# A tenth 2 MB home for the expert weights in a hybrid attention/RWKV/MoE step, with the residual reloaded elsewhere

## The reference, cut to what matters

```python
x = x + mixed @ w_out                                  # residual 1, after attention + RWKV-7 branches
h = rmsnorm(x, ln2)
logits = h @ w_router + b_router ; top 4 of 32 experts, softmax over the 4
for each expert e:
    gu = h_e @ w_gate_up[e] + b_gate_up[e]             # 1024 x 2048 weights, 8 MB
    act = (clip(up) + 1) * (min(gate, 7) * sigmoid(1.702 * min(gate, 7)))
    y_e = act @ w_down[e] + b_down[e]                  # 1024 x 1024 weights, 4 MB
x = x + sum of gate_e * y_e
y = rmsnorm(x, ln_f)
```

## Time and profile before

| what | value |
|---|---|
| runs | 1280.0, 1279.75, 1284.23 us |
| the profiled execution's own time | 1278.74 us |
| its span in the profile | 1276.9 us |
| granted TensorE clock, mean | 0.998 of full speed |
| PE busy | 1204.8 us (94%) |
| bytes moved | 458.76 MB |

### The profile page before, as it was taken

One profiled execution on the slowest core, in us unless ns is written; L12 is line 12 of the kernel. 1 busy time (PEld: TensorE's weight loads), 2 busy tenths in 40 slices (PEclk: granted clock), 3 DMA queues, 4 the chain that ended last, 5 costly groups with the idle time before them and its releaser, 6 DMA issues.

```text
span 1276.9 us, 18583 instructions
## 1 busy us (share of the span) xinstructions
PE 1204.8 (94%) x7592; PEld 590.1 (46%) x7592; DVE 339.3 (27%) x655; ACT 208.3 (16%) x421; POOL 87.0 (7%) x64
## 2 busy tenths in 40 slices
PE   6999999999999999999998989999898989898997
PEld 5877789875543433434333333324242433333332
DVE  1068497566411111111111111011111111111102
ACT  3133253320310110111011001000110101010002
POOL 0161003711000000000000000000000000000001
PEclk9999999999999999999999999999999999999999
DMA  9879450158699999999999999999999999999994
GB/s 318 196 249 300 141 210 12 37 191 339 272 379 428 428 427 429 428 426 428 428 429 425 429 428 427 427 428 429 427 428 428 428 428 428 427 428 427 428 427 185
DMA packets 52656, 458.76 MB, mean 359 GB/s; under 512 B 7092, under 2 KB 10844, under 8 KB 28004
## 3 DMA queue, kind: packets, MB, share of 16 engines
q1 hardware_dynamic: 49972, 452.22, 86.2%
q0 software_dynamic: 1824, 5.12, 1.7%
q10 hardware_dynamic: 784, 0.28, 0.1%
HBM read 453.74 MB, written 3.82 MB: 358 GB/s over the span
## 4 chain that ended last, share of the span: by engine, by line
PE 60%; DMA 29%; DVE 6%; ACT 2%; POOL 1%; issue 1%; SPq 0%; DVEq 0%; ACTq 0%; POOLq 0%
DMA ring<-in_w_gate_up 29%; PE ps L1902 24%; PE ps L1409 8%; PE ps L1923 7%; PE ps L1835 6%; PE ps L1882 3%; PE ps L1740 2%; PE ps L1844 2%; DVE work L904 2%; PE ps L1911 1%; DVE ring L904 1%; PE ps L1385 1%; PE ps L1727 1%; DVE ring L949 1%; PE ps L1657 1%
## 5 line engine op out<-in xcount | busy, mean ns | idle before, releaser
L1902 PE MATMUL ps<-ring,work 128*64 128x512 f32 x1456 | 326.5, 596 | 32.8 <-DMA ring<-in_w_gate_up 30.8
L1902 PEld LDWEIGHTS ps<-ring,work 128*64 128x64 f32 x1456 | 100.9, 137 | 236.9 <-issue 190.7
L1299 DVE TENSOR_SCALAR work<-ps 128x512 f32<-128x512 f32 x32 | 22.1, 692 | 529.0 <-PE ps L1902 529.0
L1409 PE MATMUL ps<-work,ring 128*128 128x264 f32 x672 | 156.4, 392 | 2.3 <-ACT work L552 2.2
L1902 PE MATMUL ps<-work 128*64 128x512 f32 x592 | 132.7, 594 | 11.6 <-DMA work<-in_w_gate_up 11.6
L1409 PEld LDWEIGHTS ps<-work,ring 128*128 128x128 f32 x672 | 127.5, 192 | 28.1 <-issue 6.2
L1923 PE MATMUL ps<-ring,work 128*64 128x512 f32 x608 | 137.3, 597 | 0.0
L1923 PE MATMUL ps<-work 128*64 128x512 f32 x416 | 93.3, 593 | 0.6 <-DMA work<-in_w_down 0.6
L1317 DVE SCALAR_TENSOR_TENSOR work<-work 128x512 f32<-128x512 f32 x32 | 24.0, 752 | 240.9 <-ACT work L775 240.9
L1902 PEld LDWEIGHTS ps<-work 128*64 128x64 f32 x592 | 42.4, 137 | 95.2 <-issue 88.9
L1923 PEld LDWEIGHTS ps<-ring,work 128*64 128x64 f32 x608 | 41.2, 137 | 92.7 <-issue 90.5
(11 more groups left out here) (276 smaller groups left out, 889.8 us busy)
## 6 DMA issues: line engine op xcount, KB each, us to landing
ring<-in_w_gate_up SPq DMA_DIRECT2D x91, 2048.0 KB, 36.3
ring<-in_w_down SPq DMA_DIRECT2D x38, 2048.0 KB, 40.1
work<-in_w_gate_up SPq DMA_DIRECT2D x37, 2048.0 KB, 36.8
work<-in_w_down SPq DMA_DIRECT2D x26, 2048.0 KB, 39.2
ring<-in_w_in SPq DMA_DIRECT2D x5, 3072.0 KB, 16.4
ring<-in_w_out SPq DMA_DIRECT2D x1, 4096.0 KB, 14.1
ring<-in_w_in SPq DMA_DIRECT2D x2, 1536.0 KB, 9.0
ring<-in_cache_k SPq DMA_DIRECT2D x16, 192.0 KB, 7.5
```

The source lines that it names most:

```text
L1299: v.tensor_scalar(gt, PS[BG][:, :], LIMIT, None, ALU.min).then_inc(S_("gt"), 1)
L1409: last_ = mm(psum(job, T), w, hT[:, k, :], start=k == 0, stop=k == KD - 1)
L1902: last = mm(PS[bnk][g * 64:g * 64 + 64, :], lhs, UNIT[n % 9][:, w0 + base + g * 512:w0 + base + (g + 1) * 512], start=False, stop=k == KD - 1)
```

## The change

The constants are packed: those that the expert part still needs come first (520 columns), and `before` is loaded late by POOL. The small vectors that the expert part needs move to WORK 17352. This makes room for a tenth home, WORK 520 to 4616. `acc` and the last home move to WORK 4616 to 8712. There `acc` overlaps the branch gates `sgT`, so x can't be loaded into it early: POOL loads x into `h2` (WORK 10184) instead, once `obT` is complete and all seven early stores (`st_out`, now with `pwkv` among them) have landed, and `residual` reads x from `h2` and writes `acc`. Homes 3 and 4 are given free at c == 3, homes 5 and 6 after `mb7` ahead of `wo2`. `ebias` becomes 512 columns on four groups of 32 partitions, overlaps the sample rows of `h2`, and is loaded after their transposes (`ht21`). `lnfb` goes to home 2's columns and is loaded by SP behind the last unit, when unit 182 is used up. PE's 16 pairs are written out with no inner loop; SP's loop is 3 times 5 pairs and one more. Several semaphores are shared to save their number, with no other order. The diff, cut to its core:

```diff
-CONST_NAMES = ["ident", "ones", "head_sum", "head_mean", "lo8", "up8", "up16", "up32", "strict", "incl",
-               "neg_incl", "before", "slots", "idstack", "quad"]
+CONSTS = (("ident", 128), ("ones", 128), ("slots", 128), ("idstack", 64), ("quad", 72), ("head_sum", 128), ("head_mean", 128),
+          ("lo8", 128), ("up8", 128), ("up16", 128), ("up32", 128), ("strict", 128), ("incl", 128), ("neg_incl", 128), ("before", 128))
+KEPT = 520
+EARLY = 1672
+HOMES = 10
 
...
+        starts = [sum(w for _, w in CONSTS[:i]) for i in range(len(CONSTS))]
+        C = {n: view(WORK, at, w) for (n, w), at in zip(CONSTS, starts)}
+        C["before"] = view(WORK, 24320, 128)
+        assert starts[5] == KEPT and starts[-1] == EARLY
+        sm = [EARLY]
...
-        UNIT = [view(RING, 4096 * 5, 4096), view(RING, 4096 * 2, 4096), view(RING, 4096 * 3, 4096), view(RING, 4096 * 4, 4096),
-                view(WORK, 13256, 4096), view(WORK, 24504, 4096), view(RING, 0, 4096), view(RING, 4096, 4096),
-                view(WORK, 2792, 4096)]
-        acc = view(WORK, 2792, NM, D)
-        ebias = view(WORK, 8168, FE)
-        gsamp = view(WORK, 6984, PASSES * NE)
-        accs = view(WORK, 7144, 512)
-        lnfb = view(WORK, 18600, D)
-        wr = view(WORK, 9192, KD, NE)
-        brow_r = view(WORK, 9448, NE)
+        UNIT = [view(RING, 4096 * 5, 4096), view(RING, 4096 * 2, 4096), view(RING, 4096 * 3, 4096), view(WORK, KEPT, 4096),
+                view(WORK, 13256, 4096), view(RING, 4096 * 4, 4096), view(WORK, 24504, 4096), view(RING, 0, 4096),
+                view(RING, 4096, 4096), view(WORK, 4616, 4096)]
+        acc = view(WORK, 4616, NM, D)
+        gsamp = view(WORK, 8712, PASSES * NE)
+        accs = view(WORK, 8872, 512)
+        late = [17352]
+
+        def kept(n):
+            v = view(WORK, late[0], n)
+            late[0] += n
+            assert late[0] <= 17576
+            return v
+
+        eps2, sq2, rs2, lss2, most, thr, marks = [kept(n) for n in (1, 3, 3, 1, 1, PASSES, PASSES)]
+        lnfb = view(RING, 12288, D)
+        wr = view(WORK, 24032, KD, NE)
+        brow_r = view(WORK, 24288, NE)
         h2 = view(WORK, 10184, NM, D)
         h2T = view(WORK, 17576, KD, T)
         ln2b = view(WORK, 20448, D)
@@ -325,7 +336,8 @@
         place = places(12232, 13256)
         selgT_e = [place(256), selgT]
...
+        ebias = place(512)
+        pick_e = [pick, view(WORK, 9384, SLOT)]
         npass = sb("npass", 1, I32)
...
-            load(WORK[:, 128:128 * len(CONST_NAMES)], A["c_mats"][:, 128:], "ld_mats")
+            load(WORK[:, 128:EARLY], A["c_mats"][:, 128:EARLY], "ld_mats")
...
-            for m in range(2):
-                load(acc[:, m, :], A["x_prompt"][0, m * 128:(m + 1) * 128, :], "ld_acc")
-            load(acc[:NB, 2, :], A["x_sample"][:, 0, :], "ld_acc")
...
-                        sp.dma_start(UNIT[n % 9], src).then_inc(S_(f"ld_u{n % 9}"), 16)
-
-            with sp.Fori(0, 5) as t:
-                load_pairs(3, sp.snap(t * 6), sp.snap(t * 36))
+                        sp.dma_start(UNIT[n % HOMES], src).then_inc(S_(f"ld_u{n % HOMES}"), 16)
+
+            with sp.Fori(0, 3) as t:
+                load_pairs(5, sp.snap(t * 10), sp.snap(t * 60))
             load_pairs(1, 30, 180)
...
+            sp.wait_ge(S_("unit_used"), sp.snap(passes * (6 * NE) + (HOMES + 183 - 6 * NE)))
+            load(lnfb, A["ln_f"].unsqueeze(0).broadcast_to([128, D]), "ld_lnf")
...
-                          wkvn[:64].rearrange("p c (a k) -> p c a k", a=2)).then_inc(S_("st_wkv"), 16)
+                          wkvn[:64].rearrange("p c (a k) -> p c a k", a=2)).then_inc(S_("st_out"), 16)
...
-            act.wait_ge(S_("st_wkv"), 16)
+            act.wait_ge(S_("st_out"), 16 * 7)
...
+            pool.wait_ge(S_("obT"), 4)
+            pool.wait_ge(S_("st_out"), 16 * 7)
+            for m in range(2):
+                load(h2[:, m, :], A["x_prompt"][0, m * 128:(m + 1) * 128, :], "ld_acc")
+            load(h2[:NB, 2, :], A["x_sample"][:, 0, :], "ld_acc")
             pool.wait_ge(S_("mix"), KD)
             load(ln2b, A["ln2"].broadcast_to([128, D]), "ld_ln2")
+            load(C["before"], A["c_mats"][:, EARLY:EARLY + 128], "ld_router")
             load(wr.rearrange("p (u j) e -> p u j e", j=2), A["w_router"][0].rearrange("(u p j) e -> p u j e", p=128, j=2), "ld_router")
             load(brow_r, A["b_router"].broadcast_to([128, NE]), "ld_router")
-            for i in range(2):
-                load(ebias[i * NE:(i + 1) * NE, :], A["b_gate_up"][0, :, i * FE:(i + 1) * FE], "ld_ebias")
             pool.wait_ge(S_("moe_zero"), 1)
             for g in range(2):
                 load(yS[g * 64:g * 64 + NE, :], A["b_down"][0, :, g * 512:(g + 1) * 512], "ld_bdown")
-            pool.wait_ge(S_("xgT_out"), 1)
-            load(lnfb, A["ln_f"].unsqueeze(0).broadcast_to([128, D]), "ld_lnf")
+            pool.wait_ge(full[bank["ht21"]], turn["ht21"])
+            for i in range(2):
+                for g in range(2):
+                    load(ebias[(2 * i + g) * NE:(2 * i + g + 1) * NE, :], A["b_gate_up"][0, :, i * FE + g * 512:i * FE + (g + 1) * 512], "ld_ebias")
             pool.wait_ge(S_("st_sh"), 32)
...
+                x = lambda g: h2[:n, m, g * 512:(g + 1) * 512]
                 if m == 2:
                     take(dve, "wo2")
                     for j in range(4):
-                        ins = tt(a(j % 2), PS[bank["wo2"]][32 * j:32 * j + n, :], a(j % 2), ALU.add)
+                        ins = tt(a(j % 2), PS[bank["wo2"]][32 * j:32 * j + n, :], x(j % 2) if j < 2 else a(j % 2), ALU.add)
                         V.free(ins, "wo2") if j == 3 else V(ins)
                 else:
                     for g in halves:
                         take(dve, f"wo{m}{g}")
-                        V.free(tt(a(g), psum(f"wo{m}{g}", 512, parts=n), a(g), ALU.add), f"wo{m}{g}")
+                        V.free(tt(a(g), psum(f"wo{m}{g}", 512, parts=n), x(g), ALU.add), f"wo{m}{g}")
 
...
+                if c == 3:
+                    pe.sem_inc(S_("unit_used"), 2)
...
+            after(pe, "mb7")
+            pe.sem_inc(S_("unit_used"), 2)
...
-            after(pe, "ma7", "mb7")
-            pe.sem_inc(S_("unit_used"), 3)
...
                 for i, g in ((0, 0), (1, 1), (0, 1), (1, 0)):
-                    q = slice(i * NE, (i + 1) * NE)
-                    mm(PS[(BG, BU)[i]][g * 64:g * 64 + 64, :], pick[q, :], ebias[q, g * 512:(g + 1) * 512], start=True, stop=False)
+                    q = slice((2 * i + g) * NE, (2 * i + g + 1) * NE)
+                    mm(PS[(BG, BU)[i]][g * 64:g * 64 + 64, :], pick[q, :], ebias[q, :], start=True, stop=False)
 
...
-                        pe.wait_ge(S_(f"ld_u{n % 9}"), landed[n % 9 >= 3] + 16 * (n // 9 + 1))
+                        pe.wait_ge(S_(f"ld_u{n % HOMES}"), landed[n % HOMES >= 2] + 16 * (n // HOMES + 1))
...
-                with pe.Fori(0, 2) as t:
-                    landed = [pe.snap(p * 352 + t * 128), pe.snap(p * 336 + t * 128)]
-                    for i in range(6):
-                        expert_pair(i, pe.snap(p * 16 + t * 6 + i), landed)
-                landed = [pe.snap(p * 352 + 256), pe.snap(p * 336 + 256)]
-                for i in range(4):
-                    expert_pair(i, pe.snap(p * 16 + 12 + i), landed)
+                landed = [pe.snap(p * 320), pe.snap(p * 304)]
+                for i in range(NE // 2):
+                    expert_pair(i, pe.snap(p * (NE // 2) + i), landed)
```

More of the change, by code:

```diff
@@ L721, in _ @@
             rms2(2)
-            A_(nc.scalar.activation(lss[:1], eps[:1], ACT.Exp))
+            A_(nc.scalar.activation(lss2[:1], eps2[:1], ACT.Exp))
             h2_T(1)
@@ L757, in _ @@
             act.wait_ge(S_("npass"), 1)
-            nc.scalar.activation(lss[:1], lss[:1], ACT.Copy).then_inc(S_("y_out"), 1)
+            nc.scalar.activation(lss2[:1], lss2[:1], ACT.Copy).then_inc(S_("y_out"), 1)
             passes = act.value_load(npass[0:1, 0:1], min_val=1, max_val=PASSES)
@@ L797, in _ @@
                     A_.ready(nc.scalar.activation(h2[:, m, g * 512:(g + 1) * 512], PS[BA[m][g]][:, :], ACT.Square,
-                                                  accum_out=sqh[:, m, 0:1] if g == 0 else sq1[:, m:m + 1]), "sq_half", 2 * m + g + 1)
+                                                  accum_out=sqh[:, m, 0:1] if g == 0 else sq2[:, m:m + 1]), "sq_half", 2 * m + g + 1)
                 act.wait_ge(S_("sq_sum"), m + 1)
-                A_.ready(nc.scalar.activation(rs1[:, m:m + 1], sq1[:, m:m + 1], ACT.Sqrt, bias=sqh[:, m, 1:2], scale=1.0 / D), "rms3", m + 1)
+                A_.ready(nc.scalar.activation(rs2[:, m:m + 1], sq2[:, m:m + 1], ACT.Sqrt, bias=sqh[:, m, 1:2], scale=1.0 / D), "rms3", m + 1)
                 if m == 0:
                     act.wait_ge(S_("samp_ms"), 1)
-                    A_.ready(nc.scalar.activation(rss, PS[BX][:, 0:1], ACT.Sqrt, bias=eps, scale=1.0 / D), "samp_rms", 1)
```

(17 more changed lines are left out.)

82 lines of the change are left out of this document (38 added, 44 removed).

## The result

| kernel | median us (runs) | ratio to the kernel before | 95% interval |
|---|---|---|---|
| before | 1280.0 (7) | | |
| after | 1288.57 (7) | 1.0063 | 1.0041 to 1.0084 |

The change makes the kernel **8.1 us slower** (1280.0 x 0.0063; by the interval 5.2 to 10.8). The median of 1288.57 is just over the upper end of the range, 1288. The forecast was 3.9 us slower.

What follows compares the result with a forecast made beforehand. PE's jobs were taken as the bound up to about 351 us, then the weight stream at 427 GB/s. Profiled, 1278.74 - 4.9 (home) + 8.8 (late x) = 1282.6 us; for the median 1280.0 + 3.9 = 1283.9 us, range 1275 to 1288.

Steps and rivals of the forecast that it cites:

- The tenth home, -4.9 us: Unit stream: ten units have landed when the first is used up, 182 instead of 183 follow; gain 4.9 us.
- The edits at nothing: Written-out PE pairs, SP's loop, `lnfb` behind the last units, a DVE `memset`, bias products: together no change in time.
- The store of `pwkv` at 300 us, x at 319.8 us: Before the residual: the store lands about 7 us later, POOL then issues x, which takes 15.5 us beside the stream.
- the price of a turn: DMA engines alternate small rows with the stream's 16 KB rows: 0.8 us per row of x, 0.63 us per completion.
- `ln2b` by 324 and not the last: POOL's queue behind x: `ln2b` arrives by about 324 us, before h2's norm needs it.
- PE 8.8 us late: Transposes of h2: h2 is ready at 326.6 us, where PE began them at 317.78 without a gap.
- All behind them is 8.8 us late: After h2's transposes: PE works in order, so homes 7 to 9 and the first expert shift by the same 8.8 us.
- x in time: First rival, at the residual: x lands early enough, the home's gain stands alone, 1275.1 us; chance 0.22.
- x last: Second rival: x lands at 323 us when SP's queue is dry, PE 12.0 us late, 1287.1 us; chance 0.13.
- the home brings nothing: Third rival, unit stream: the continuous stretch does not start one unit ahead, 8.8 us are left, 1288.8 us; chance 0.04.

Runs made afterwards that it cites:

- Run 5: The kernel after with homes 3 to 6 released together after `wo2`, and SP waiting for one release more, so only nine units are under way: 1283.74 us, 1.0012.
- filled kernels: The kernel after with useless 128x512 matmuls where PE waits before the transposes of h2: nine 1.0064, ten 1.0043 and 1.0029 of the kernel before.
- Run 4: The kernel after with ACT's store of `pwkv` issued directly behind its evacuation: 1280.91 us, 0.9988 of the kernel before.
- the filling with nine: The kernel after with nine 128x512 matmuls, results overwritten, where PE waits before the transposes of h2: 1291.58 us, 1.0064 of the kernel before.
- runs 1, 2 and 6: The kernel after with homes 3 to 6 released after `wo2` (1: 0.9955; repeated in 6: 0.9945), x on SP's queue (2: 0.9951), both with `ln2b` on SP (6: 0.9949).
- cured kernels: The kernel after with homes 3 to 6 released after `wo2` (0.9955, 0.9945), x on SP's queue (0.9951), or both with `ln2b` on SP (0.9949).

## Why the prediction was wrong

Point by point, by its own steps:

- **The tenth home, -4.9 us: right.** From the first expert to the end it was 1276.9 - 351.24 = 925.66 us and is now 1294.7 - 374.26 = 920.44, so 5.2 us less. Run 5 isolates the home at 4.6 in the profiles.
- **The edits at nothing: right within what the timed runs can tell.** The stream's rate is as before and `lnfb` is covered. PE's one wait of 2.0 us for issue is gone. The profile of run 5 leaves 1.0 to 1.5 us to these edits, which the prediction put at nothing; that is not settled.
- **The store of `pwkv` at 300 us, x at 319.8 us: right, the second number partly by luck.** x was issued at shifted 301.2, so the store was 1.2 us later than forecast. x then needed 18.6 us from its first issue to its last landing and not 19.8, and landed at shifted 319.8. The second half of `x_prompt` landed 6.3 us behind the first, where eight turns of 0.8 and a completion of 0.63, 7.0 us, were priced. So the price of a turn, taken from `pwkv` and `b_down`, held within a tenth for x, eight times the bytes of `pwkv`, and the two errors cancel. The Trainium skill ("DMA: Bandwidth & Descriptors", Queues, rings and completion order) has an engine drain a whole packet before it switches queues. The prediction worked from it that x would come when the stream has run out, and the trace does not show that: x had landed at 330.6 us, and unit 6, the last of the seven, at 316.5 + 19.6 = 336.1. But that working, like the one for `b_down`, gave the stream a whole packet and the small transfer a single row in each turn. With whole packets on both sides they would need fewer turns, and the runs here do not decide between rows and packets.
- **`ln2b` by 324 and not the last: slightly wrong.** It landed at shifted 325.4 and released the norm after 2.01 us. In the filled kernels ACT's root did so after 1.70 us, so this cost 0.3 us. Run 4 shows that `ln2b` is the next wait once x comes sooner.
- **PE 8.8 us late: right as a wait, 9.16 us.**
- **"All behind them is 8.8 us late": here it failed.** The first expert is 374.26 - 10.83 - 351.24 = 12.2 us late. The missing 3 us are the output projection's half behind h2, 10.09 instead of 7.13 us. The step took every matmul behind the wait at the duration it has in the kernel before. So the slower clock behind a wait was put at nothing without a reason. The three profiles of the kernel after have 10.09, 9.88 and 9.80, the three filled ones 7.13. Of the timed runs two pairs agree (3.1 and 3.5 us) and the filling with nine does not. The Trainium skill has this price ("TensorE: Matmul & The Clock Gate", Terms): the time at the slower clock times the share of the clock withheld. Worked out here, 16 matmuls of 7.13 us that took 10.09 spent twice the 3.0 us, some 6 us from 338.9, at 1.2 GHz, which agrees with a trace whose granted clock is 0.50 at 339 to 344 us and 1.00 from 346. The prediction did not apply it.

With it the sum is -5.2 + 12.2 = +7.0 us, and measured are +8.1 with 5.2 to 10.8. The last 1.1 us are inside that interval and are not assigned to anything.

Of the rivals, x in time is what runs 1, 2 and 6 made of the kernel: it was priced at 1275.1 us, a ratio of 0.9962, and they gave 0.9945 to 0.9955 with that value in each interval. x last did not happen, although the time came out near its price of 1287.1 us: PE was 12 us late, but by a wait of 9.2 and 3 us of slow clock. That agreement is luck. That the home brings nothing is ruled out by run 5.

## What to carry to other kernels

A home released early is not a gain by itself. If all homes fill up anyway before the next bound, the earlier units only lie in the queues beside something small that is needed now. Put a needed small load ahead of the deep stream in its own queue, or hold the stream back until it has been issued. Then look for the next small load in line: here it was `ln2b`. And when a change makes PE wait for longer than it does today, price the matmuls behind the wait at the slower clock too. Here 9 us of idle time were followed by 3 us more.

## What the runs showed of the hardware

- **Idle time of PE costs clock.** In the kernel after the granted clock was 0.50 at 332 to 337 us, while PE stood still and before any matmul resumed, and 16 matmuls then took 10.09 us instead of 7.13. After a wait of only 1.58 us in run 4 they still took 8.83, in one profile; there the clock fell after the matmuls had resumed at 330.7 us (1.00 at 329 to 331, 0.50 at 333 to 335). In the filled kernels waits of 0.35 to 1.21 us left them at 7.13.
- **Beside a deep queue a transfer took three to four and a half times its own time.** 512 KB of x landed in 4.1 us on idle DMA engines and in 13.4 us beside the stream of 16 KB rows (the mean of its two halves). `ln2b`, 512 KB behind x, took 4.5 and 20.3 us.
- **Open: the stretch before `w_out`.** Its issue came at 272.23 and 277.65 us in the two profiles of the kernel before, and at 278.2 to 284.9 in those of the changed kernels. PE's waits there come and go. This is the kernel before, run again, PE's waits from 90 to 278 us (us in total, times, longest); the wait for L943 was 0.9 us in its first profile:

```profile
PE ps L1385 <- DVE work L943: 4.1, 2, 3.6
```

  And this the kernel after, same stretch:

```profile
PE ps L1591 <- DVE ring L921: 4.6, 1, 4.6
PE ps L1403 <- DVE work L960: 3.9, 2, 3.5
```

  The first kind belongs to no kernel. The second, 2.2 to 4.8 us in every profile of a changed kernel, is at most 0.5 us in the two profiles of the kernel before, and may belong to the new layout. The cured kernels gained in the timed runs all that the stretch behind `w_out` gives them (1004.9 - 999.0 = 5.9 us, or 0.0046), so it shows no price there. No run tried it by itself.
